# Hybrid decoder step: wide products for the cached values, four value buffers, and the weight remainders moved to VectorE

## The reference

```
h    = rms_norm(x, g_mix_pre);  proj = h @ w_in          # 3584 columns
rec  = gated linear recurrence (4 heads, state 128x128)   # prompt from 0, samples from state_hgrn
attn = softmax over three dilated windows, T5 bias, 8 heads of 64
x    = x + rms_norm(concat(norm(rec)*gate, norm(attn)) @ w_out, g_mix_post)
u    = square(relu(rms_norm(x, g_mlp_pre) @ w_up))        # 4096 columns
x    = x + rms_norm(u @ w_down, g_mlp_post)
```

## Time and profile before

| what | value |
|---|---|
| time, median of 3 runs | 1785.26 us (1781.99 to 1786.69) |
| the profiled execution, its own time | 1770.3 us |
| its span, first to last instruction | 1768.5 us |
| PE busy | 1675.9 us, 95% of the span |
| DVE, ACT, POOL busy | 820.3, 833.0, 768.9 us |
| DMA queue q1 | 43.7% of 16 engines |
| mean granted TensorE clock | 0.955 |

### The profile page before, as it was taken

The page is one execution under the profiler, slowest core; times in us unless marked ns, Lnnn a source line. Parts: engine busy times, 40 slices in busy tenths (PEclk is TensorE's granted clock), DMA queues, the critical chain, the costliest instruction groups (busy, mean ns, idle before and its releaser), DMA issues.

```text
span 1768.5 us, 30432 instructions
## 1 busy us (share of the span) xinstructions
PE 1675.9 (95%) x12404; PEld 1610.1 (91%) x12404; DVE 820.3 (46%) x1337; ACT 833.0 (47%) x1488; POOL 768.9 (43%) x449
## 2 busy tenths in 40 slices
PE   3999999989999999999889999999899999999995
PEld 2998889988999999999789987899889999999995
DVE  4754433676426722113887443245854266211164
ACT  4535433347554655345454452333574646551451
POOL 4430101311058788557763101022200778883674
PEclk9999877999999999999899997789999999999997
DMA  5554442435245465434333543314343545563442
GB/s 168 180 160 127 175 155 72 133 112 167 96 144 166 143 188 184 130 106 155 123 120 120 175 177 99 139 63 144 129 150 108 155 153 158 181 186 100 131 144 89
DMA packets 76997, 247.82 MB, mean 140 GB/s; under 512 B 8723, under 2 KB 18195, under 8 KB 76732
## 3 DMA queue, kind: packets, MB, share of 16 engines
q1 hardware_dynamic: 76860, 245.89, 43.7%
HBM read 234.04 MB, written 14.44 MB: 141 GB/s over the span
## 4 chain that ended last, share of the span: by engine, by line
PE 81%; DVE 10%; DMA 3%; ACT 2%; issue 2%; POOL 1%; SPq 0%; POOLq 0%; ACTq 0%; DVEq 0%
PE ps L932 60%; PE ps L929 5%; PE ps L996 3%; PE ps L1185 3%; DVE square_sum L1243 2%; DVE reg L1268 2%; DMA vc<-vc 1%; DVE w_rest L1230 1%; PE ps L1125 1%; PE ps L1112 1%; PE ps L1140 1%; DVE reg L1283 1%; PE ps L1072 1%; PE ps L1180 1%; DVE norm_every L1253 1%
## 5 line engine op out<-in xcount | busy, mean ns | idle before, releaser
L602 POOL TENSOR_TENSOR w_rest<-w_raw,w_high 128x1024 fp32r<-128x1024 f32 x240 | 586.2, 2448 | 229.7 <-ACT w_high L681 229.2
L932 PE MATMUL ps<-h_high,w_rest 128*128 128x320 f32 (+1 forms) x1920 | 589.1, 307 | 27.6 <-POOL h_rest L662 8.0
L932 PE MATMUL ps<-h_rest,w_high 128*128 128x320 f32 (+1 forms) x1920 | 577.1, 301 | 0.0
L932 PE MATMUL ps<-h_high,w_high 128*128 128x320 f32 (+1 forms) x1920 | 576.7, 300 | 0.0
L681 ACT ACTIVATE w_high<-w_raw 128x1024 fp32r<-128x1024 f32 x384 | 402.0, 1051 | 243.4 <-PE ps L932 243.4
L932 PEld LDWEIGHTS ps<-h_high,w_rest 128*128 128x128 f32 x1920 | 374.0, 195 | 36.2 <-issue 22.5
L932 PEld LDWEIGHTS ps<-h_rest,w_high 128*128 128x128 f32 x1920 | 374.1, 195 | 0.4
L932 PEld LDWEIGHTS ps<-h_high,w_high 128*128 128x128 f32 x1920 | 373.4, 195 | 0.0
L932 PE MATMUL ps<-u_high,w_rest 128*128 128x320 f32 (+1 forms) x1024 | 307.4, 300 | 11.2 <-DVE u_rest L1328 8.5
L932 PE MATMUL ps<-u_rest,w_high 128*128 128x320 f32 (+1 forms) x1024 | 305.0, 298 | 0.0
L932 PE MATMUL ps<-u_high,w_high 128*128 128x320 f32 (+1 forms) x1024 | 304.8, 298 | 0.0
(11 more groups left out here) (171 smaller groups left out, 2023.7 us busy)
## 6 DMA issues: line engine op xcount, KB each, us to landing
w_raw<-w SPq DMA_DIRECT2D x384, 512.0 KB, 3.6
kc<-kcT SPq DMA_DIRECT2D x16, 512.0 KB, 6.3
vc<-vc SPq DMA_DIRECT2D x16, 512.0 KB, 6.2
s_in<-s SPq DMA_DIRECT2D x8, 512.0 KB, 4.6
ss<-s_in SPq DMA_DIRECT2D x8, 512.0 KB, 5.2
bias<-rel_scratch SPq DMA_DIRECT2D x8, 512.0 KB, 4.7
rel_scratch<-rel_row SPq DMA_DIRECT2D x1, 2560.0 KB, 11.5
bias<-rel_scratch SPq DMA_DIRECT2D x8, 256.0 KB, 5.3
```

Of the source, the lines that this page charges most:

```text
L602: V.tensor_tensor(wlo[:, v % RING], raw[:, v % RING], whi[:, v % RING].bitcast(F32), ALU.subtract).then_inc(S["w_lo_p"], 1)
L932: last = pe.matmul(ps[:, bank, 0:n], wt[:, slot, c, :], xt[:, c, :], **flags)
```

## The change

- `s_pv` on TensorE now takes the weights as the stationary operand and moves the values 512 columns wide: four products of 64 output rows (two slices of the cached rows for two sequences) and one of 128 output rows for the own rows. Each of the 128 result rows (sequence, head, token) then holds all 512 value columns.
- VectorE multiplies that with a 0/1 mask `head_mask`, which keeps the row's own head, into one of two tiles `mo`. A new step `s_sel`, one block later, has four small products of `mo` with a 0/1 matrix `tok_sel`, which bring it to the old layout; ScalarE copies once.
- The cached values have four buffers. Both of the first two pairs are loaded at block 0 of IB, and the others two pairs ahead.
- `lo_engine` is gone: VectorE makes all remainders but the first four, which stay on POOL. Of these, POOL makes one before and three after the first `h_rest`.
- The tokens of half 0 are loaded in four DMAs, and ScalarE starts squaring at the first.
- The states of the first two recurrence heads are loaded five blocks later (`state_in`, IA 25), one into another place; `a_sq`, `a_sum` and `a_spr` of half 0 stand one block later. The other small products stay where they were.

```diff
-def lo_engine(o):
-    if o.ph == "IA":
-        return "pool" if o.i < 8 else "dve"
-    return "dve" if o.ph in ("IB", "OA", "U0A", "D0A") else "pool"
...
-    put("IA", 20, "state_in", 0)
-    put("IA", 20, "state_in", 1)
+    put("IA", 25, "state_in", 0)
+    put("IA", 25, "state_in", 1)
...
+    put("IB", 0, "vc_in", 1)
     for p in range(HP):
+        put("IB", 5 + 2 * p, "s_sel", p)
         put("IB", 4 + 2 * p, "s_pv", p)
...
-            put("IB", 4 + 2 * p, "vc_in", p + 1)
         if p + 2 < HP:
+            put("IB", 4 + 2 * p, "vc_in", p + 2)
...
-    put("IB", 11, "a_sq", 0)
+    put("IB", 12, "a_sq", 0)
...
+    head_of_row = ((row % 64) // TB)[:, None] == np.arange(HA)[None]
+    tok_of_row = (row // 64 * TB + row % TB)[:, None] == np.arange(2 * TB)[None]
...
-            sp.dma_start(x[:, :, 0:WIDE[0]], xT[:, :, 0:WIDE[0]]).then_inc(S["x_in0"], 16)
+            for c in range(0, KC, 2):
+                sp.dma_start(x[:, c:c + 2, 0:WIDE[0]], xT[:, c:c + 2, 0:WIDE[0]]).then_inc(S[f"x_part{c // 2}"], 16)
...
             def vc_in(l, p):
-                if p:
-                    sp.wait_ge(S["spv_done"], HP * l + p)
+                if p > 1:
+                    sp.wait_ge(S["spv_done"], HP * l + p - 1)
                 else:
                     sp.wait_ge(S["blk"], by[l, "IA", 31].n + 1)
+                    sp.wait_ge(S["s_max"], 3 * (unit(l, 0, 7) + 1))
...
@@ gpsimd
-            for v in range(RING):
-                rest(v)
...
+            rest(0)
             for p in range(4):
                 pre(0, 0, 0, p)
+            for v in range(1, RING):
+                rest(v)
...
@@ scalar
-            def s_pv(l, p):
-                act.wait_ge(S["spv_done"], HP * l + p + 1)
-                for s in range(2):
...
+            def s_sel(l, p):
+                act.wait_ge(S["sel_done"], HP * l + p + 1)
+                A.activation(ao[0][:, :, 16 * p:16 * p + 16], ps[:, 7, 0:64].rearrange("p (j t) -> p j t", j=HP), ACT.Copy)\
+                    .then_inc(S["so_there"], 1)
...
@@ tensor
             def s_pv(l, p):
                 pe.wait_ge(S["spt_there"], n + 1)
                 for s in range(2):
-                    pe.wait_ge(S[f"vc_in{s}"], 16 * (n + 1))
+                    pe.wait_ge(S[f"vc_in{p % 2}{s}"], 16 * (2 * l + p // 2 + 1))
+                take(7)
+                for k2 in range(2):
+                    for s in range(2):
+                        q0 = k2 * P + 64 * s
+                        pe.matmul(ps[64 * s:64 * s + 64, 7, :], pts[:, q0:q0 + 64], vcs[p % 2][s][:, k2, :],
+                                  start=(k2 == 0), stop=False)
+                pe.matmul(ps[:, 7, :], pts[0:TS, 256:384], va[0][0:TS, 2, :], start=False, stop=True).then_inc(S["spv_done"], 1)
+                held[7] = (S["mo_set"], n + 1)
+
+            def s_sel(l, p):
+                pe.wait_ge(S["mo_set"], n + 1)
                 take(7)
                 for j in range(HP):
...
+                    last = pe.matmul(ps[:, 7, 16 * j:16 * j + 16], mo[p % 2][:, j * P:j * P + P], tok_sel, start=True, stop=True)
...
@@ vector
+            def s_pv(l, p):
+                dve.wait_ge(S["spv_done"], n + 1)
+                V.tensor_tensor(mo[p % 2][:].rearrange("p (h d) -> p h d", h=HA), ps[:, 7, :].rearrange("p (h d) -> p h d", h=HA),
+                                head_mask.unsqueeze(2).broadcast_to([P, HA, DH]), ALU.mult).then_inc(S["mo_set"], 1)
...
-                late = [v + RING for v in free_at[o.n] if lo_engine(o) == "dve" and v + RING < n_loads]
+                late = [v + RING for v in free_at[o.n] if v + RING < n_loads]
```

More of the change, by code:

```diff
@@ L162, in steps_at @@
             put("IB", 1 + 2 * p, "kc_in", p + 1)
[L163 removed]
         if p + 2 < HP:
+            put("IB", 4 + 2 * p, "vc_in", p + 2)
             put("IB", 2 + 2 * p, "q_big", p + 2)
[L166 to L169 removed]
+    put("IB", 12, "a_sq", 0)
+    put("IB", 13, "a_sum", 0)
+    put("IB", 15, "a_spr", 0, 0)
+    put("IB", 16, "a_spr", 0, 1)
     for lv in range(LEVELS):
@@ L340, in build @@
     tmp = place("tmp", [P, 4, WIDE[0]])
-    cst = place("cst", [P, 264])
+    cst = place("cst", [P, 288])
     ones = place("ones", [P, P])
@@ L380, in build @@
     s_in = [place(f"s_in{a}", [P, NB, P], offset=o)
-            for a, o in enumerate((part(1, 8), part(1, 12), o_hh[0], part(1, 20)))]
+            for a, o in enumerate((o_f, part(1, 12), o_hh[0], part(1, 20)))]
     v_exp = place("v_exp", [P, NB, P], offset=o_hl[0])
     kc = [place(f"kc{s}", [P, HP, PAST], offset=o) for s, o in enumerate((part(0, 16), o_vt[1]))]
-    vcs = [place(f"vc{s}", [P, 2, 512], offset=o + 4 * 4 * WIDE[0]) for s, o in enumerate((o_hh[0], o_hl[0]))]
+    vcs = [[place(f"vc{i}{s}", [P, 2, 512], offset=o) for s, o in enumerate(two)]
+           for i, two in enumerate(((o_hh[0] + 16 * WIDE[0], o_hl[0] + 16 * WIDE[0]), (o_va[1], part(1, 8))))]
+    mo = [place(f"mo{i}", [P, 512], offset=o_key[1] + 2048 * i) for i in range(2)]
     prob = [place("prob0", [P, 2, 256], offset=o_key[1]), place("prob1", [P, 2, 512], offset=o_hh[1] + 4096)]
@@ L411, in build @@
     free_at = {}
-    lo_of, n_lo = {}, {"pool": 0, "dve": 0}
-    for v in range(RING):
-        n_lo["pool"] += 1
-        lo_of[v] = ("w_lo_p", n_lo["pool"])
+    lo_of = {v: ("w_lo_p", v + 1) for v in range(RING)}
     for o in outs:
@@ L889, in _ @@
             table = {"x_sq": x_sq, "norm_sum": norm_sum, "post": post, "pre": pre, "k_t": k_t, "out": out, "s_upd": s_upd,
-                     "r_sum": r_sum, "r_spr": r_spr, "sc": sc_, "pt": pt_, "pv": pv, "s_sc": s_sc, "s_pt": s_pt, "s_pv": s_pv,
-                     "a_sq": a_sq_, "a_sum": a_sum, "a_spr": a_spr}
+                     "r_sum": r_sum, "r_spr": r_spr, "sc": sc_, "pt": pt_, "pv": pv, "s_sc": s_sc, "s_pt": s_pt,
+                     "s_sel": s_sel, "a_sq": a_sq_, "a_sum": a_sum, "a_spr": a_spr}
             for o in outs:
@@ L1174, in s_pv @@
                 for s in range(2):
[L1175 removed]
+                    pe.wait_ge(S[f"vc_in{p % 2}{s}"], 16 * (2 * l + p // 2 + 1))
[8 more added lines that the diff above has]
+            def s_sel(l, p):
+                n = HP * l + p
+                pe.wait_ge(S["mo_set"], n + 1)
                 take(7)
                 for j in range(HP):
[L1178 to L1187 removed]
+                    last = pe.matmul(ps[:, 7, 16 * j:16 * j + 16], mo[p % 2][:, j * P:j * P + P], tok_sel, start=True, stop=True)
+                last.then_inc(S["sel_done"], 1)
                 held[7] = (S["so_there"], n + 1)
@@ L1217, in _ @@
                      "r_sum": r_sum, "r_spr": r_spr, "sc": sc_, "pt": pt_, "pv": pv, "s_sc": s_sc, "s_pt": s_pt,
-                     "s_pv": s_pv, "a_sum": a_sum, "a_spr": a_spr}
+                     "s_pv": s_pv, "s_sel": s_sel, "a_sum": a_sum, "a_spr": a_spr}
             for o in outs:
@@ L1537, in _ @@
                      "s_upd": s_upd, "r_sum": r_sum, "r_spr": r_spr, "q_big": q_big, "sc": sc_, "s_sc": s_sc, "s_div": s_div,
-                     "a_sum": a_sum, "a_spr": a_spr}
+                     "s_pv": s_pv, "a_sum": a_sum, "a_spr": a_spr}
             late = []
```

55 lines of the change are left out of this document (24 added, 31 removed).

## The result

| | median of 4 runs | range | ratio to before, 95% interval |
|---|---|---|---|
| before, same chip | 1785.32 us | 1781.99 to 1786.69 | |
| after | 1686.21 us | 1680.09 to 1696.66 | 0.9454 [0.9404, 0.9503] |

What follows compares the result with a forecast made beforehand. TensorE's own stream, its clock and its stalls were taken as the bound (81% of the chain). 55.7 + 13 + 30.5 - 3 = 96 us off 1770.3 gives 1674, with the 15.0 offset 1689 us; range 1666 to 1728.

Steps and rivals of the forecast that it cites:

- Sample values: Sample value products in IB: 8.5 us of work, 39.2 of clock and 8.0 of waits saved, together 55.7 us.
- work term: Value products and s_sel in IB: 31.5 us for eight pairs against 40.0 at full clock, 8.5 us saved.
- rival 4: Wide s_pv: the two array halves do not overlap, 16 us more, 1705 us; chance 0.07.
- clock term: s_pv and blocks behind: low clock costs 45.2 us, 6 us left lost (bounds 0 and 45.2), 39.2 gained.
- rival 1: IB: clock falls all the same, as narrow state-update products and s_sel remain; 39 us missing, 1728 us; chance 0.11.
- The burst at IB 0: Loads at block 0 of IB: 1 MB more ahead of the next keys, no wait expected, at most 8.0 us back.
- The start: Blocks 0 and 1: earlier tokens and POOL's reordered remainders end block 1 at 26.5, not 39.45; 13 us (bounds 8 and 15).
- Remainders: Weight remainders on VectorE: 20 us at layer 0's end, 7.5 at the very end, 3 mid-layer; 30.5, less 3 for delays.
- Rival 2: Where two layers' norms meet: moving remainders to VectorE turns collisions into queueing; 30.5 us missing, 1720 us; chance 0.12.
- can just keep pace: U3B and D3B: VectorE would have 46.7 us of work against 46.1 us of blocks.
- VectorE's busy time: Whole kernel, a sign of being right: VectorE near 1080 us busy.
- Rival 3: MLP blocks: VectorE's order becomes the bound, 118 remainders of 1.22 us exposed, 144 us, 1833 us; chance 0.02.

Runs made afterwards that it cites:

- e6: Kernel before with only the wide value products, mask, s_sel and moved steps; two buffers, old start, remainders as before: 1737.75 us, ratio to before 0.9749.
- e10: Changed kernel with the eight state products of each state update placed one at a time between matmuls of IB blocks 3 to 6: 1670.36 us, ratio 0.9377.
- e3: Changed kernel with the value products narrow again, no mask and no s_sel, four buffers kept: 1720.25 us, ratio to before 0.9677.
- e8: Changed kernel without the eight products of 8 columns in each s_upd (64 in all): 1666.5 us, ratio to before 0.9340.
- e1: Changed kernel with weight remainders back on POOL in IA 0 to 7, OB, U0B to D3B: 1722.36 us, ratio to before 0.9653.
- e5: Kernel before with only the weight remainders, all but the first four, moved to VectorE: 1754.75 us, ratio to before 0.9833.
- e12: e10 with second pair's values asked for behind its keys, plus every second remainder of U3B and D3B on POOL: 1682.19 us, ratio to before 0.9425.
- e9: The changed kernel itself, measured again without any change: 1686.79 us, ratio to before 0.9463.

## Why the prediction was right, and where it was not

**The total.** 1689 against 1686.2, but two errors cancel in it. Against the profiled execution the terms came to 96 us and the spans differ by 85.6. And the offset of 15.0 us to the median was carried over to a kernel whose profiled execution lies only 1.5 us under its median. The execution of before that was profiled had a clock of 0.955; 28 later ones had 0.945 to 0.956, mostly 0.948. It had lost less to the clock than most: 0.955 - 0.948 is 0.7% of the span, an estimated 12 of the 15 us. So most of the offset was itself clock, and the profiled execution of the changed kernel shows no such offset.

**Sample values, forecast 55.7 us: 48.7 in the profiles** (52.5 in the table's column, less the 3.8 us of `a_spr`). The parts came differently. The work term was right (3.73 us a pair for 3.94, so 10.2 us for 8.5), and the halves overlap, which puts rival 4 out. The waits went, though e6 shows that more than half of them goes without buffers. The clock term was mis-sized: 48.7 - 10.2 - 8.0 leaves 30.5 us for it, not 39.2. The windows show where. After, the two stretches of IB lost 0.11 x 126.1 + 0.06 x 108.2 = 20 us to the low clock where 6 were left; before, they had lost 0.17 x 144.8 + 0.22 x 137.2 = 55 us, and the forecast had counted 45.2, since it looked only at the value products and the blocks behind them. By these windows the change won back some 35 us of clock, by subtraction 30.5. "I leave 6 us lost" rested on one run at full rate. Layer 1 of the same trace has the opposite: the clock falls right behind a state update, before any value product.

```profile
1055.68 1.95 PE L1066 MATMUL ps<-reg,s_in 128*128 128x8 f32 x16
1057.57 2.91 PE L1072 MATMUL ps<-v_exp,ks_tok 64*128 64x512 f32 x4
...
1061.23 3.68 PE L1155 MATMUL ps<-kc,qbig 128*64 128x256 f32 x16
```

So rival 1's doubt, that narrow state products still open each run, was partly true: by e10 standing there in a row they still cost 16 us. By the medians, e3 gives 34 us (40 by the ratio) for the narrow form in all, work and clock, for the 8.5 + 39.2 of the forecast.

What the Trainium skill says in "TensorE: Matmul & The Clock Gate", section "HAM oscillation — how this bites in real kernels", that gaps lower the clock, is shown too, by the wait before 186.42 in e8, in which the clock fell with TensorE idle. It is only part of the matter here: with it alone e10 should have gained nothing.

**The burst at IB 0, forecast no wait:** 0.5 us. Right, but only just: the state products were the cover, and e8 shows the price without it, 7.1 us. Masking takes VectorE 0.69 us each, and no wait for it is in TensorE's list.

**The start, forecast 13 us:** 10.0 at the place that it named, the end of block 1 (39.45 to 29.40), and 11.5 by block 8. Block 0 started where it should (17.53). It ended at 25.4 and not 23: POOL's `h_rest` slices run at 0.96 to 1.28 us each beside VectorE, not 3.33/4, and block 0 follows them with its matmuls 0.27 us apart, against 0.15 us from 26 us on. And the step named only two causes; by e1 and e5, some 6 of the 11.5 us come only because the remainders of IA's first blocks left POOL as well.

**Remainders, forecast 30.5 - 3: 26.5 by place** (15.8 + 7.1 + 3.6), plus those 6. Rival 2 is out by e1, e5 and e12. At the end of layer 0 83.1 us stand for the 79 forecast: that VectorE "can just keep pace" was too kind. It falls behind in U3B, until TensorE waits 2.42 us for `u_rest` early in D3B; the clock of D3B is 0.94 (in e9, the same kernel, it stayed at full rate there, and the three stages took 81.5 us). One thing was not counted: a remainder on VectorE collides as well, with the odd sums of `x` that stayed on POOL. Timelines of VectorE and of POOL after, in U3B:

```profile
811.33 1.90 DVE L1232 TENSOR_TENSOR w_rest<-w_raw,w_high 128x1024 fp32r<-128x1024 f32 x1
...
814.82 1.21 DVE L1232 TENSOR_TENSOR w_rest<-w_raw,w_high 128x1024 fp32r<-128x1024 f32 x1
```
```profile
811.09 1.06 POOL L656 TENSOR_TENSOR x<-x,reg 128x320 f32<-128x320 f32 x1 [237.93 <-DVE reg L1270]
814.58 2.94 POOL L656 TENSOR_TENSOR x<-x,reg 128x320 f32<-128x320 f32 x1 [2.42 <-DVE reg L1270]
```

Of such a pair one is longer: the remainder by 0.7 us, or the sum by 1.9 us, and the squares wait for the sum.

**VectorE's busy time, forecast near 1080: 960.** Only the long operations of U3B and D3B were looked at; u_rest and the sums of squares of the whole MLP were long as well, 154 us in all, mostly off the path. **Rival 3** is out: no wait for an eviction appeared, and 0.4 us for `reg` is all there is.

## What to carry to other kernels

Small products that stand in a row between large ones are dear twice: one of 8 columns takes 0.235 us and one of 16 columns 0.255, and a row of them can halve the clock for what comes behind, with TensorE never idle. Make them wide by exchanging the roles of the operands, as the change does; where that can't be done, put them one at a time among the wide matmuls (16 us here, at no work saved). And before sharing elementwise work between VectorE and POOL, compare the mean duration of the same line beside and without the other engine: here moving 236 operations to the busier engine made that engine's other work 154 us shorter.

## What the runs showed of the hardware that was not expected

- Three kinds of products at full clock, fp32, from start to start: 64 state products of 8 columns, eight in 1.88 us (0.235 each); four of 64 rows and 128 columns 0.59; four of 64 rows and 512 columns 1.87. Four times the width costs 3.2 times as much (0.59 to 1.87); for the own rows, of 128 output rows, 2.6 times (0.41 to 1.05).
- A row of state products stands before the fall of the clock and not behind it: 1.88 us in seven of eight cases of the changed kernel, granted clock 1.00 (181.73 and 194.23 among them), while L1070 behind them takes 1.9 us or up to 3.7. What such a row costs at half clock no run shows. The narrow value products of the kernel before did take longer there: 1.25 and 2.38 us for ten records.
- A remainder on POOL stretches even a tiny VectorE operation to its own length: in the start of the changed kernel an operation on 128x8 takes 2.30 us beside one (row below) and 0.17 us otherwise.

```profile
23.06 2.30 DVE L1546 TENSOR_TENSOR lb<-lb,lbc 128x8 f32<-128x8 f32 x1
```
